# Three orders of work in a two-layer RWKV-7 and differential-attention trunk: lambda's sums, key totals and decays, norm rows, and an attention pipeline with four buffers

## The reference

```python
def rwkv7_time_mix(h, ...):                 # 16 heads of 64
    xr, xw, xk, xv, xa, xg = (h + dx * mix[i] for i in range(6))   # dx = h_prev - h
    r = xr @ w_rkvo[0]; k = xk @ w_rkvo[1]; v = xv @ w_rkvo[2]
    w_log = -softplus(-(w0 + tanh(xw @ w1) @ w2)) - 0.5
    decay = exp(-exp(w_log));  a = sigmoid(a0 + (xa @ a1) @ a2);  g = sigmoid(xg @ g1) @ g2
    kk = heads(k * k_k);  kk = kk / max(sqrt(sum(kk * kk)), 1e-12)
    k = k * (1 + (a - 1) * k_a)
    y = rwkv7_recurrence(r, decay, k, v, -kk, kk * a)
    y = (y - mean) * rsqrt(var + 64e-5) * ln_w + ln_b
    y = (y + sum(r * k * r_k) * v) * g
    return y @ w_rkvo[3]

def diff_attention(h, k, v, ...):           # 8 heads, two maps of 64 each, values of 128
    lam_full = exp(sum(lam[0]*lam[1])) - exp(sum(lam[2]*lam[3])) + lambda_init
    q = rmsnorm(h @ w_q)                    # per head and map
    logits = q @ k^T / 8 + t5_bias, causal; probs = softmax(logits)
    attn = probs[:, 0] - lam_full * probs[:, 1]
    o = rmsnorm(attn @ v, subln_g) * (1 - lambda_init)
    return o @ w_o
```

## Time and profile before

| | us |
|---|---|
| timed runs: median of 3 (lowest to highest) | 1588.63 (1588.36 to 1589.49) |
| profiled execution | 1585.8 |
| its span | 1584.0 |
| PE busy | 1486.4 (94%) |
| DVE busy | 734.9 (46%) |
| ACT busy | 589.3 (37%) |
| POOL busy | 604.3 (38%) |

### The profile page before, as it was taken

How to read it: one execution, slowest core, us unless ns; L and a number is a source line. 1 busy time by engine, 2 the same in 40 slices (tenths; PEclk the granted TensorE clock), 3 DMA queues, 4 the chain that set the end, 5 groups by cost and what they waited for, 6 DMA issues and landing times. The chain is left out here.

```text
span 1584.0 us, 23537 instructions
## 1 busy us (share of the span) xinstructions
PE 1486.4 (94%) x9095; PEld 1173.5 (74%) x9095; DVE 734.9 (46%) x1134; ACT 589.3 (37%) x928; POOL 604.3 (38%) x326
## 2 busy tenths in 40 slices
PE   4799998888999999999999999979999999999998
PEld 4566777785687888888877677645778888888876
DVE  4866978846653300232148763576553200332143
ACT  5745434645332211232244333367233211232252
POOL 5342332222244443434433333333143444444432
PEclk9999999999999999999999999989999999999999
DMA  5212200031123233232232332200023233233231
GB/s 138 85 53 80 80 27 2 10 110 55 53 80 101 85 107 119 80 106 93 94 115 80 111 103 80 78 29 1 27 80 107 87 101 117 81 105 106 79 107 54
DMA packets 123502, 126.97 MB, mean 80 GB/s; under 512 B 8332, under 2 KB 120204, under 8 KB 123416
## 3 DMA queue, kind: packets, MB, share of 16 engines
q1 hardware_dynamic: 122720, 124.51, 24.3%
q0 software_dynamic: 320, 0.66, 0.2%
q10 hardware_dynamic: 376, 0.61, 0.1%
HBM read 123.64 MB, written 2.12 MB: 79 GB/s over the span
## 5 line engine op out<-in xcount | busy, mean ns | idle before, releaser
L461 POOL TENSOR_TENSOR wlo<-wraw,whi 128x1024 fp32r<-128x1024 f32 x108 | 262.5, 2430 | 795.0 <-ACT whi L1329 782.2
L557 PE MATMUL pb<-xh,whi 128*128 128x512 f32 x1184 | 474.1, 400 | 17.7 <-DVE xl L1848 7.4
L558 PE MATMUL pb<-xl,whi 128*128 128x512 f32 x1184 | 463.4, 391 | 0.0
L559 PE MATMUL pb<-xh,wlo 128*128 128x512 f32 x1184 | 463.4, 391 | 0.0
L1329 ACT ACTIVATE whi<-wraw 128x2048 fp32r<-128x2048 f32 (+1 forms) x111 | 209.3, 1885 | 223.0 <-PE pb L559 222.9
L557 PEld LDWEIGHTS pb<-xh,whi 128*128 128x128 f32 x1184 | 223.6, 189 | 89.7 <-issue 33.3
L464 POOL TENSOR_TENSOR wlo<-wraw,whi 128x1024 fp32r<-128x1024 f32 x111 | 274.9, 2476 | 23.6 <-ACT whi L1329 12.4
L558 PEld LDWEIGHTS pb<-xl,whi 128*128 128x128 f32 x1184 | 223.8, 189 | 48.0 <-issue 3.4
L559 PEld LDWEIGHTS pb<-xh,wlo 128*128 128x128 f32 x1184 | 223.5, 189 | 47.9
L557 PE MATMUL pb<-hid_h,whi 128*128 128x512 f32 x512 | 199.3, 389 | 0.0
L559 PE MATMUL pb<-hid_h,wlo 128*128 128x512 f32 x512 | 199.2, 389 | 0.0
(11 more groups left out here) (285 smaller groups left out, 1732.7 us busy)
## 6 DMA issues: line engine op xcount, KB each, us to landing
wraw<-in_mlp_w_dram SPq DMA_DIRECT2D x128, 512.0 KB, 4.3
wraw<-in_rwkv_w_rkvo_dram SPq DMA_DIRECT2D x32, 512.0 KB, 4.3
wraw<-in_ple_w_gate_dram SPq DMA_DIRECT2D x16, 512.0 KB, 3.9
xtok<-in_x_dram SPq DMA_DIRECT2D x8, 512.0 KB, 6.1
wraw<-in_w_k_shared_dram SPq DMA_DIRECT2D x8, 512.0 KB, 4.4
wraw<-in_w_v_shared_dram SPq DMA_DIRECT2D x8, 512.0 KB, 4.4
wraw<-in_diff_w_q_dram SPq DMA_DIRECT2D x8, 512.0 KB, 4.0
wraw<-in_diff_w_o_dram SPq DMA_DIRECT2D x8, 512.0 KB, 4.3
```

What stands on the lines that cost most here:

```text
L461: pool.tensor_tensor(wlo[:, par, front], wraw[:, par, front], whi[:, par, front].bitcast(F32), ALU.subtract)
L557: mm(o, wh, ah, start=first, stop=False)
L558: mm(o, wh, al, start=False, stop=False)
L559: return mm(o, wl, ah, start=False, stop=last)
```

## The change

In the front, lambda's sums move ahead of DVE's first reciprocal; ACT's Exp moves into the key stage ahead of the decays; DVE finishes `lamf` after the receptance mixes. ACT takes the second key block after five of eight decays. The key totals 6 and 7 move one k-step later in block 8, and spreads 1 and 2 share one place. `high(N_WO, 1)` moves behind the group norm's Sqrt, and five of eight `x_turn` behind `rstd_rows`. Five of the eight splits for the query blocks move ahead of the evacuation of the last value block. Attention gets four buffers for `Lg` and `Pr`, turns and products come one sub-block later, totals are made four heads at a time on four column groups, the reciprocal for the last queries moves from i = 3 to i = 1, block N_DO + 1 is rounded at i = 10 and its low part made behind the loop, and the broadcasts use 32 rows each, six ahead of the projection and two in front of k-step 1.

```diff
-            lows(N_KS + 2, N_DO + 2)
+            lows(N_KS + 2, N_DO)
+            low(N_DO, 0, slice(0, 2048), False)
...
-                if i >= 8 and i % 4 == 0:
-                    h = (i - 8) // 4
+                if i >= 9 and i % 4 == 1:
+                    h = (i - 9) // 4
...
-            lows(N_DO + 2, N_DO + 4)
+            lows(N_DO + 1, N_DO + 3)
+            low(N_DO + 3, 1, slice(0, 2048), False)
...
+            def kk_two(c):
+
+                def f():
+                    kk_spread(c)()
+                    kk_spread(c + 1)()
+                return f
...
-                     3: {3: kk_total(4), 4: kk_total(5)}, 4: {3: kk_total(6), 4: kk_total(7), 5: kk_spread(0), 6: kk_spread(1), 7: kk_spread(2)},
+                     3: {3: kk_total(4), 4: kk_total(5)}, 4: {4: kk_total(6), 5: kk_total(7), 6: kk_spread(0), 7: kk_two(1)},
...
-            for c in range(2, 6):
-                x_turn(c)
+            x_turn(2)
             pe.wait_ge(s.gn_rs, 1)
             rstd_rows(0)
-            x_turn(6)
-            x_turn(7)
             pe.wait_ge(s.bon_v, CT)
             rstd_rows(2)
+            for c in range(3, CT):
+                x_turn(c)
...
-            def head_total(h):
-
-                pe.wait_ge(s.o_sq, h + 1)
-                mm(pb[7][0:8, :], one_col[:, 8 - h:16 - h], tmp[:, h % 2, :], start=(h == 0), stop=(h == 7)).then_inc(s.o_ps, 1)
+            def head_totals(g):
+
+                pe.wait_ge(s.o_sq, 4 * g + 4)
+                for q in range(4):
+                    ins = mm(pb[7][32 * q:32 * q + 32, :], one_col[:, 1 - g:33 - g], tmp[:, q, :], start=(g == 0), stop=(g == 1))
+                ins.then_inc(s.o_ps, 1)
...
-                mm(pb[4 + h % 4][:, :], ident[:, h:h + 1].to_broadcast([P, P]), rstd[:, :], start=True, stop=True)\
-                    .then_inc(s.ob_ps, 1)
+                q, g = h % 4, h // 4
+                r = slice(32 * q, 32 * q + 32)
+                mm(pb[O_BANK[h]][:, :], ident[r, 32 * q + g:32 * q + g + 1].to_broadcast([32, P]), rstd[r, :],
+                   start=True, stop=True).then_inc(s.ob_ps, 1)
...
-                if 0 <= i - 3 < 32:
-                    attn_turn(i - 3)
-                if i >= 4:
-                    values(i - 4)
-                if i >= 12 and i % 4 == 0:
-                    head_total((i - 12) // 4)
-            head_total(6)
-            head_total(7)
+                if 0 <= i - 4 < 32:
+                    attn_turn(i - 4)
+                if i >= 5:
+                    values(i - 5)
+                if i == 23:
+                    head_totals(0)
+            head_totals(1)
...
-            for h in range(4):
+            for h in range(6):
                 head_rstd(h)
-            proj(N_DO, X_O, 96, {k: (lambda h=k + 4: head_rstd(h)) for k in range(4)})
+
+            def last_rstd():
+                head_rstd(6)
+                head_rstd(7)
+            proj(N_DO, X_O, 96, {1: last_rstd})
...
             high(2, 0)
-            act.wait_ge(s.lam_s, 1)
-            A(lamw[:, 2:4], lamw[:, 0:2], ACT.Exp).then_inc(s.lam_e, 1)
...
                     if t == 0:
-                        for c in range(CT):
+                        act.wait_ge(s.lam_s, 1)
+                        A(lamw[:, 2:4], lamw[:, 0:2], ACT.Exp).then_inc(s.lam_e, 1)
+                        for c in range(5):
+                            decay_before(c)
+                    if t == 1:
+                        for c in range(5, CT):
                             decay_before(c)
...
                 square(c)
-                if c == 3:
-                    high(N_WO, 1)
             act.wait_ge(s.gn_ps, 2)
             A(rstd[:, :], pb[7][:, :], ACT.Sqrt, bias=eps_g, scale=1.0 / HD).then_inc(s.gn_rt, 1)
+            high(N_WO, 1)
...
                 high(N_VS + b + 1, (b + 1) % 2)
+                if b == 3:
+                    splits(V_N10, 8 * (N_VS + 3), 0, 5)
...
-            splits(V_N10, 8 * (N_VS + 3))
+            splits(V_N10, 8 * (N_VS + 3), 5)
...
-            high(N_DO + 1, 1)
             for i in range(1, 32 + 4):
                 if i - 1 < 32:
                     exps(i - 1)
-                if 0 <= i - 3 < 32:
-                    attn_copy(i - 3)
-                if i >= 8 and i % 4 == 0:
-                    head_take((i - 8) // 4)
+                if i == 10:
+                    high(N_DO + 1, 1)
+                if 0 <= i - 4 < 32:
+                    attn_copy(i - 4)
+                if i >= 9 and i % 4 == 1:
+                    head_take((i - 9) // 4)
...
-            act.wait_ge(s.rows_0, 1)
-            A(rstd[0:8, :], pb[7][0:8, :], ACT.Sqrt, bias=eps_n[0:8, :], scale=1.0 / P).then_inc(s.o_rt, 1)
+            A(rstd[:, :], pb[7][:, :], ACT.Sqrt, bias=eps_n, scale=1.0 / P).then_inc(s.o_rt, 1)
...
+            dve.wait_ge(s.lam_in, 16)
+            link(tt(lrow[:, 0:2, :], lrow[:, 0:4:2, :], lrow[:, 1:4:2, :], ALU.mult))
+            dve.tensor_reduce(lamw[:, 0:2], lrow[:, 0:2, :], AX.X, ALU.add).then_inc(s.lam_s, 1)
             dve.wait_ge(s.x_rt, 1)
             dve.reciprocal(x_rms, x_rms).then_inc(s.x_rs, 1)
...
             mixes(4, MIX_R)
+            dve.wait_ge(s.lam_e, 1)
+            link(tt(lamf, lamw[:, 2:3], lamw[:, 3:4], ALU.subtract))
+            link(ts(lamf, lamf, LAMBDA_INIT, None, ALU.add))
             kk_invert(0)
...
-            for i in range(32 + 2):
+            for i in range(32 + 3):
                 if i < 32:
                     logits(i)
-                if i >= 2:
-                    combine(i - 2)
-                if i == 3:
+                if i >= 3:
+                    combine(i - 3)
+                if i == 1:
                     dve.wait_ge(s.qk_rt, 13)
                     dve.reciprocal(rstd[:, :], rstd[:, :]).then_inc(s.qk_rs, 1)
```

More of the change, by code:

```diff
@@ L181, in trunk @@
         lamf = small[:, 87:88]
-        st_n, st_l, st_r = (small[:, 116 + 6 * k:122 + 6 * k] for k in range(3))
+        st_n, st_l, st_r = (small[:, 134 + 8 * k:142 + 8 * k] for k in range(3))
         lamw = small[:, 108:112]
@@ L185, in trunk @@
         qk_gain = small[:, 161:162]
-        one_col = small[:, 162:178]
+        one_col = small[:, 184:217]
         St = at("St", ST, [P, 5, CT, S])
@@ L242, in trunk @@
         OT = at("OT", ST, [P, TT, D])
+        O_BANK = (4, 5, 6, 7, 2, 3, 4, 5)
         pb = [ctx.enter_context(nc.psum_tensor(f"pb{i}", [P, S], F32)) for i in range(8)]
@@ L540, in _ @@
                         pool.wait_ge(s.qk_n, 16)
-                    if h >= 2:
-                        pool.wait_ge(s.o_ps, h - 1)
-                    pool.tensor_tensor(tmp[:, h % 2, :], QT[:, h, :], QT[:, h, :], ALU.mult).then_inc(s.o_sq, 1)
-            lows(N_DO + 2, N_DO + 4)
+                    if h >= 4:
+                        pool.wait_ge(s.o_ps, 1)
+                    pool.tensor_tensor(tmp[:, h % 4, :], QT[:, h, :], QT[:, h, :], ALU.mult).then_inc(s.o_sq, 1)
+            lows(N_DO + 1, N_DO + 3)
+            low(N_DO + 3, 1, slice(0, 2048), False)
             lows(L_MLP[1], L_MLP[1] + 32)
@@ L1262, in head_rstd @@
             def head_rstd(h):
-                if h >= 4:
-                    pe.wait_ge(s.o_f, h - 3)
-                mm(pb[4 + h % 4][:, :], ident[:, h:h + 1].to_broadcast([P, P]), rstd[:, :], start=True, stop=True)\
-                    .then_inc(s.ob_ps, 1)
+                if h >= 6:
+                    pe.wait_ge(s.o_f, h - 5)
+                q, g = h % 4, h // 4
+                r = slice(32 * q, 32 * q + 32)
+                mm(pb[O_BANK[h]][:, :], ident[r, 32 * q + g:32 * q + g + 1].to_broadcast([32, P]), rstd[r, :],
+                   start=True, stop=True).then_inc(s.ob_ps, 1)
             pe.wait_ge(s.v_ev, 8)
-            for i in range(32 + 4):
+            for i in range(32 + 5):
                 if i < 2:
@@ L1758, in exps @@
                 act.wait_ge(s.lg, 2 * i + 2)
-                if i >= 3:
-                    act.wait_ge(s.at_rdy, i - 2)
+                if i >= 4:
+                    act.wait_ge(s.at_rdy, i - 3)
                 for m in range(2):
-                    k = 2 * (i % 3) + m
-                    A(Pr[i % 3][:, m, 0:w], Lg[i % 3][:, m, 0:w], ACT.Exp, bias=st_n[:, k:k + 1], scale=-1.0,
+                    k = 2 * (i % 4) + m
+                    A(Pr[i % 4][:, m, 0:w], Lg[i % 4][:, m, 0:w], ACT.Exp, bias=st_n[:, k:k + 1], scale=-1.0,
                       accum_out=st_l[:, k:k + 1]).then_inc(s.pexp, 1)
@@ L1779, in head_take @@
                 if h >= 6:
-                    act.wait_ge(s.o_ps, h - 1)
+                    act.wait_ge(s.o_ps, 1)
                     act.wait_ge(s.o_sq, h)
-                    A(tmp[:, h % 2, :], pb[5 + h % 2][:, :], ACT.Square).then_inc(s.o_sq, 1)
+                    A(tmp[:, h % 4, :], pb[5 + h % 2][:, :], ACT.Square).then_inc(s.o_sq, 1)
             act.wait_ge(s.qk_ps, 16)
             A(rstd[:, :], pb[6][:, :], ACT.Sqrt, bias=eps_n, scale=1.0 / HD).then_inc(s.qk_rt, 1)
-            high(N_DO + 1, 1)
```

(24 more changed lines are left out.)

16 lines of the change are left out of this document (8 added, 8 removed).

## The result

The changed kernel takes 1573.68 us (median of four runs, 1571.60 to 1577.77) against 1589.06 for the kernel before: ratio 0.9906, interval 0.9886 to 0.9927. The forecast was 1569.9 us, range 1561 to 1578. The profiled execution took 1573.53 us (before 1585.8). The measured time lies nearer to those of rival 2 (1574.7) and rival 3 (1575.1) than to the forecast, so only the traces can tell which account holds.

What follows compares the result with a forecast made beforehand. TensorE, busy 1486.4 of 1584.0 us, bounds the kernel, so gains come only from its idling, its clock after idling, or less work. Terms +0.8 -6.5 +4.5 -2.9 -3.7 -8.3 -2.6 = -18.7 from 1588.6 give 1569.9 us, range 1561 to 1578.

Steps and rivals of the forecast that it cites:

- rival 2: Attention: ACT sets the pace, so it gains 4 instead of 8.3 us, table load costs 1.3; 1574.7 us, chance 0.15.
- rival 3: First three terms: decays' gain shifts POOL's halves into DVE's work, +4 instead of -1.2 us; 1575.1 us, chance 0.10.
- the second key block: Evacuation after five decays: PE's 3.61 us wait goes and 2.9 us lost to the clock return, -6.5 us.
- the front: Lambda: Exp's table load goes, Tanh needs its own load of 1.28 us, +0.8 us.
- Rival 4: Attention: PE's clock stays at the low level, about +30 us; 1600 us, chance 0.05.
- rival 1: Key totals: POOL's halves miss DVE, so the term is -2.0 us; 1563.4 us, chance 0.20.
- Key totals: Last totals a step later: POOL's halves meet DVE's SBUF operations, second reciprocal 3.5 us later, +4.5 us.
- 2 us for that: Key totals: clock loss expected after PE's 6.7 us wait for the reciprocal, 2 us.
- Norm stage: Recurrence's norm: weight copy leaves the squares (2.2 us reach the Sqrt), PE sends first rows before other transposes, -2.9 us.
- their copies end at 393.3, ACT splits only then: Norm stage: five late transposes' copies delay ACT's split; DVE's first low part ends at 394.6, 2.9 us earlier.
- Attention and hand-over: Attention's start, totals and four buffers -8.3 us, hand-over to the output projection -2.6 us; together -10.9 us.
- the clock falls for less: -1.0: Attention's start: PE idles 4.7 instead of 8.0 us, so the low clock of 0.50 lasts less, -1.0 us.

Runs made afterwards that it cites:

- the half late: Changed kernel, with POOL's halves of the projection's second weights waiting for the last combined attention block: 1569.43 us, 0.9876.
- held halves: Changed kernel, with two of POOL's weight pieces in the receptance blocks held until DVE's second and fourth prep: 1567.34 us, 0.9875.
- the spins of attention's start: Kernel with both edits, plus five spins behind the fourth pair of scores and one before the first turn: 1563.58 us, 0.9852.
- the best kernel: Kernel with both edits, the spins of attention's start, two spins in the second MLP, and six instead of eight spins before the broadcasts: 1560.37 us, 0.9830.
- early totals: Changed kernel, with the last two key totals and three spreads back at the k-steps of the kernel before: 1568.94 us, 0.9875.
- both edits: Changed kernel with early totals and the half late together: 1566.03 us, 0.9864.

## Why the prediction was right or wrong

**Right, by mechanism and size:** the second key block (-6.45 for -6.5, and -6.5 alone), the front (Tanh's own table load, +0.5 for +0.8), the query block (-4.1 for -3.7), and the copy in the norm stage (-2.24 for -2.2). In attention the steady period of a head fell from 8.24 to 7.18 us, by about the one total of the earlier trace rows; there PE is busy 7.04 of 7.20 us and ACT 6.59, so rival 2 (ACT paces) falls. Rival 4 falls too: the clock was back to 1.00 well before the steady part. So does rival 1, as the pieces did meet DVE, though its price was right: held off DVE, they give -2.1 in this stage for its -2.0. Rival 3 falls, as the gain of the decays was kept.

**Key totals, a term that was mis-sized** (+4.5, measured +5.85). The forecast had the reciprocal 3.5 us later and a wait of 6.7; they are 3.2 and 6.3. What failed is "2 us for that", the clock. The third receptance block grew by 10.2 us (14.0 to 24.2), of which the wait explains 5.8; the other 4.4 are the clock, 0.65 over the next 15.6 us. 1.7 came back in the next two blocks, where PE had waited before (forecast 1.0). I had taken less than the 2.9 us that the clock cost after 3.6 us in the earlier trace rows, for a wait nearly twice as long; it cost more. The +5.85 is also taken against an execution of the kernel before in which the block with the seventh total took 19.5 us; against the 21.0 of other traces it would be 1.5 less. In the five traces with late totals and unheld pieces the stage grew by 5.3 to 6.7 us. I also left out that the one-input `TENSOR_SCALAR` can be held (1.84 instead of 0.54). The Trainium skill, page "SBUF — State Buffer", section "Who interferes with whom", names it among the operations that can take the shared pair of ports; the trace agrees.

**Norm stage, mis-sized** (-2.9, measured -4.0). The order of PE was put at 0.7 and is worth 1.7. The step that failed is "their copies end at 393.3, ACT splits only then": that is 12.0 us behind the Sqrt as forecast, and they ended 11.1 behind it; DVE had its first low part at 12.3 instead of 13.3.

**Attention and hand-over, the main miss** (-10.9, measured -5.25). Two steps failed. The first is what the change leaves behind the loop: I counted the halves' going as a gain at attention's start and did not ask what they would meet at the end. There the half holds the last combine, and in this execution the clock fell as well: 4.2 us, of which 2.6 are what most traces show and the rest is this execution's. The second is "the clock falls for less: -1.0". It fell for as long as before, 0.50 over the next 7.8 us, because PE still idled 3.5 and 1.0 us; the wait only moved from the turn to the scores. It costs 3.5 us in all, by the spins. With the half late, attention up to the last product gives -7.5 (forecast -8.3, which holds the -1.0 that never came), and the hand-over -2.0 (forecast -2.6). In the changed kernel itself the stretch from the first scores to the last product is 76.9 us against 81.7, 4.8 less. The prediction called itself wrong if this were under 5, so by its own sign its account of attention failed; with the half late it is 74.2.

**Not foreseen:** +1.9 in the second MLP. PE waits there for POOL's piece for the third block, 1.88 us instead of 1.52, and the clock falls to 0.66 over the next 5 us. Counted from the start of a block 25 us earlier, PE's steps up to that wait lie at the same places in both traces. What differs is DVE, behind its reciprocal at the head of its loop, the kernel before and then the changed one:

```profile
1175.53 3.35 DVE L1843 RECIPROCAL rstd<-rstd 128x512 f32<-128x512 f32 x1 [4.84 <-ACT rstd L1342]
1179.11 1.29 DVE L2200 TENSOR_TENSOR tmp<-pb,rstd 128x512 f32<-128x512 f32 x2 [0.23 <-DVE rstd L1843]
...
1161.05 3.35 DVE L1867 RECIPROCAL rstd<-rstd 128x512 f32<-128x512 f32 x1 [4.84 <-ACT rstd L1359]
1164.99 1.29 DVE L2220 TENSOR_TENSOR tmp<-pb,rstd 128x512 f32<-128x512 f32 x2 [0.58 <-PE pb L563]
```

DVE goes on 0.35 us later, and ACT's copy and POOL's piece follow it. It is so in all eleven traces with the changed order on DVE and in none of the three with the old one; why is not shown. In the three kernels with 1.52 to 1.54 us the first half of the MLP takes 177.3 us; in seven of the eight with 1.85 to 1.88 it takes 179.2, in the eighth 177.6; with spins in the wait 177.6 in all three. So the wait bears on the clock, but does not decide it alone.

The forecast sum was -18.7, the medians give -15.4. The changed kernel's own profile and that of the kernel before give -12.3, since the latter is an execution 3.3 us under its median. That the median came within 3.3 us of the forecast is in part luck. By the traces, attention and the MLP are 7.6 us worse than forecast and the key totals 1.4, while the norm stage, the query block and the unchanged scan, which only varied, are 2.6 better; and the medians lie 3.1 us further apart than the two profiles.

Not tried: held halves together with the spins of attention's start. By the traces the value blocks would come some 2 us earlier than in the best kernel. The front and the query block had no run of their own; their terms are read from the two traces alone.

## What to carry to other kernels

Before moving a shared-port operation of one engine off a wait, list what the other engine does at its new place, and do so too for those that move along because a block became shorter. A wait on the right semaphore, which holds such a piece back until the other engine has passed, gained 6.3 us here. A wait that only changes its place can keep its price in clock; a few spins in it took 3.5 us off the stage in the traces.

## What the runs showed of the hardware

One wait does not have one price. The same code with nearly the same wait gave two lengths of the block behind it, in different executions:

| Place, wait | one length (us) | the other (us) |
|---|---|---|
| Seventh key total, 2.3 us | 19.5 (5 traces) | 21.0 (3 traces) |
| Projection's first step, 1.5 us | 12.3 (9 traces) | 13.8 and 15.4 (1 each) |
| First scores to the end of the spins, last combine held 2.07 us | 82.8 (1 trace) | 84.4 (3), 86.1 (1) |

All of these go with the granted clock of that stretch: 1.00 or 0.92 in the first row; 1.00, 0.88 and 0.78 in the second; in the third it differs both behind the first turn and behind the last combine. (The best kernel, with 13.8 us, has two spins fewer ahead of that wait.) The block with the seventh total, first in the kernel with early totals, then in the one with both edits (length, busy times, clock, DMA, as above):

```profile
130.96:151.97 21.01, 18.73 (x59) 10.67 (x58) 15.72 (x23) 10.42 (x16) 4.71 (x2) 0.92 0.16 55
...
130.98:150.50 19.52, 17.25 (x60) 9.89 (x59) 15.76 (x23) 10.42 (x16) 4.70 (x2) 1.00 0.18 61
```

These differences can explain much of the 2 to 7 us between single runs of one kernel, and why small terms had to be read stage by stage. The Trainium skill, page "TensorE: Matmul & The Clock Gate", section "What's actually happening", says of the matmuls at a kernel's start that the number of slow ones varies from run to run of the same kernel. No run here was read for its start; behind waits inside the kernel the traces show such a variation too. What decides it in a given run stays open. The unchanged scan also varied, from 129.6 to 132.4 us from the start of the last value block to PE's first bonus total.

A POOL piece of 1024 columns beside DVE held each conflicting operation for the rest of the piece, and the second half of the piece got in again between two of them (2.89 and 2.86 us in a row for operations of 0.69).
